# One square per token tile over both banks, in place of one per bank, in a four-layer transformer kernel

## The reference, cut to what matters

```
x = x + rms_norm(f(rms_norm(x, g_pre)), g_post)       (some with a factor 0.5 before the second norm)
rms_norm(y, g) = y * rsqrt(mean(y*y) + 1e-6) * g      (mean over the 1024 columns)
```

## Time and profile before

| | |
|---|---|
| median of 3 runs | 1870.45 us (1869.24 to 1873.09) |
| the profiled execution | 1869.73 us |
| its span | 1867.9 us |
| PE busy | 1818.2 us, 97% of the span |
| DVE busy | 1113.2 us, 60% |
| ACT busy | 913.2 us, 49% |
| POOL busy | 73.7 us, 4% |
| mean granted clock of PE | 0.992 |

### The profile page before, as it was taken

How to read it: one execution, slowest core, us unless ns; L and a number is a source line. 1 busy time by engine, 2 the same in 40 slices (tenths; PEclk the granted TensorE clock), 3 DMA queues, 4 the chain that set the end, 5 groups by cost and what they waited for, 6 DMA issues and landing times.

```text
span 1867.9 us, 21863 instructions
## 1 busy us (share of the span) xinstructions
PE 1818.2 (97%) x8662; PEld 1513.4 (81%) x8662; DVE 1113.2 (60%) x1457; ACT 913.2 (49%) x1378; POOL 73.7 (4%) x184
## 2 busy tenths in 40 slices
PE   5998999999999999999999999999999999999998
PEld 5897888888788878888888878887888888878887
DVE  6775655776655565556566755556555666674554
ACT  4555444655444454445454444444444545454443
POOL 1001000200000010001000000001000100000000
PEclk9999999999999999999999999999999999999999
DMA  6434555634455565556455555655555655555552
GB/s 206 136 115 135 192 191 174 184 120 133 137 191 191 180 209 186 182 194 208 161 184 196 164 176 184 194 185 192 192 190 181 206 177 180 187 175 164 190 187 91
DMA packets 221206, 327.80 MB, mean 175 GB/s; under 512 B 10544, under 2 KB 156528, under 8 KB 220848
## 3 DMA queue, kind: packets, MB, share of 16 engines
q1 hardware_dynamic: 218592, 318.64, 52.3%
q0 software_dynamic: 1952, 7.67, 1.3%
q10 hardware_dynamic: 560, 0.08, 0.0%
HBM read 325.31 MB, written 1.05 MB: 175 GB/s over the span
## 4 chain that ended last, share of the span: by engine, by line
PE 96%; DVE 2%; ACT 1%; issue 1%; DMA 0%; ACTq 0%; DVEq 0%; POOLq 0%; POOL 0%
PE Dp L1714 16%; PE Dp L1716 16%; PE Dp L1715 16%; PE Gp L1714 13%; PE Gp L1716 13%; PE Gp L1715 13%; PE Tp L1773 2%; DVE wlo L1041 1%; PE Gp L1896 1%; PE Tp L1887 1%; PE Dp L1920 1%; PE Tp L1729 0%; PE Tp L1920 0%; PE Dp L1896 0%; DVE stage L1101 0%
## 5 line engine op out<-in xcount | busy, mean ns | idle before, releaser
L1041 DVE TENSOR_TENSOR wlo<-raw,whi 128x1024 fp32r<-128x1024 f32 (+1 forms) x608 | 715.0, 1214 | 367.1 <-ACT whi L614 367.0
L614 ACT ACTIVATE whi<-raw 128x1024 fp32r<-128x1024 f32 (+1 forms) x608 | 606.5, 1045 | 308.8 <-PE Dp L1716 164.3
L1714 PE MATMUL Gp<-whi,a_hi 128*128 128x512 f32 x1056 | 422.4, 400 | 19.6 <-DVE inner L1142 19.6
L1716 PE MATMUL Gp<-whi,a_lo 128*128 128x512 f32 x1056 | 414.6, 393 | 0.0
L1715 PE MATMUL Gp<-wlo,a_hi 128*128 128x512 f32 x1056 | 414.0, 392 | 0.0
L1714 PE MATMUL Dp<-whi,a_hi 128*128 128x512 f32 (+2 forms) x672 | 257.2, 383 | 14.4 <-ACT Z L757 7.0
L1716 PE MATMUL Dp<-whi,a_lo 128*128 128x512 f32 (+2 forms) x672 | 252.0, 375 | 0.0
L1715 PE MATMUL Dp<-wlo,a_hi 128*128 128x512 f32 (+2 forms) x672 | 251.4, 374 | 0.0
L1714 PEld LDWEIGHTS Gp<-whi,a_hi 128*128 128x128 f32 x1056 | 200.0, 189 | 61.3 <-DVE inner L1142 22.2
L1716 PEld LDWEIGHTS Gp<-whi,a_lo 128*128 128x128 f32 x1056 | 199.8, 189 | 43.2
L1715 PEld LDWEIGHTS Gp<-wlo,a_hi 128*128 128x128 f32 x1056 | 200.4, 190 | 39.7
(11 more groups left out here) (246 smaller groups left out, 1623.4 us busy)
## 6 DMA issues: line engine op xcount, KB each, us to landing
raw<-in_ffn_w_gate_up SPq DMA_DIRECT2D x176, 512.0 KB, 4.7
raw<-in_w_in SPq DMA_DIRECT2D x132, 512.0 KB, 4.6
raw<-in_ffn_w_down SPq DMA_DIRECT2D x88, 512.0 KB, 4.4
raw<-in_w_gate SPq DMA_DIRECT2D x44, 512.0 KB, 4.0
raw<-in_w_up SPq DMA_DIRECT2D x44, 512.0 KB, 5.0
raw<-in_w_down SPq DMA_DIRECT2D x44, 512.0 KB, 4.3
raw<-in_w_out SPq DMA_DIRECT2D x16, 512.0 KB, 4.1
raw<-in_w_pool_out SPq DMA_DIRECT2D x16, 512.0 KB, 4.3
```

Of the source, the lines that this page charges most:

```text
L614: return nc.scalar.activation(whi[g % W][0:rows, c0:c0 + n], raw[g % R][0:rows, c0:c0 + n], ACT.Copy).then_inc(hi_done, 1)
L1041: return V.tensor_tensor(wlo[g % W][0:rows, c0:c0 + n], raw[g % R][0:rows, c0:c0 + n], whi[g % W][0:rows, c0:c0 + n].bitcast(F32), ALU.sub ...
L1714: mm(o, hi, wh, start=start, stop=False, skip_group_check=True)
L1716: return mm(o, lo, wh, start=False, stop=stop, skip_group_check=True)
```

## The change

`square_y` loses its index c. It waits for `done[t]`, the end of both halves, and squares 1024 columns over both banks of the tile in one ACTIVATE with one accumulator. So there are 20 squares in place of 40. `scaled(t, 0)` and `scaled(t, 1)` both wait for this one square. POOL adds eps to the one sum and takes the power: two instructions a tile in place of three. PE's increments of `y_c0` go away. The order of the calls on every engine stays, but for the two squares that become one.

```diff
             def y_rstd(t, s):
                 eps = EPS * (4.0 if s in HALVED else 1.0)
-                pool.wait_ge(ysq[t], 2 * s + 1)
-                pool.tensor_scalar(ssy[:, 2 * t:2 * t + 1], ssy[:, 2 * t:2 * t + 1], eps, None, ALU.add
-                                   ).then_inc(ysum[t], 1)
-                pool.wait_ge(ysq[t], 2 * s + 2)
-                pool.wait_ge(ysum[t], 2 * s + 1)
-                pool.tensor_tensor(sy[:, t:t + 1], ssy[:, 2 * t:2 * t + 1], ssy[:, 2 * t + 1:2 * t + 2], ALU.add
-                                   ).then_inc(ysum[t], 1)
-                pool.wait_ge(ysum[t], 2 * s + 2)
+                pool.wait_ge(ysq[t], s + 1)
+                pool.tensor_scalar(sy[:, t:t + 1], ssy[:, t:t + 1], eps, None, ALU.add).then_inc(ysum[t], 1)
+                pool.wait_ge(ysum[t], s + 1)
                 pool.tensor_tensor(rsy[:, t:t + 1], sy[:, t:t + 1], half[:, 0:1], ALU.pow).then_inc(yrs[t], 1)
...
-            def square_y(t, c, s, last):
-                if c == 1:
-                    act.wait_ge(done[t], used(last))
-                elif s in BY_CHUNK:
-                    act.wait_ge(done[t], used(last - 2))
-                else:
-                    act.wait_ge(y_c0[t], c0_of(s))
-                i = 2 * t + c
-                nc.scalar.activation(junk[:, 512 * i:512 * i + 512], D(t, c), ACT.Square,
-                                     scale=1.0 / 16 if s in HALVED else 1.0 / 32, accum_out=ssy[:, i:i + 1]
+            def square_y(t, s, last):
+                act.wait_ge(done[t], used(last))
+                nc.scalar.activation(junk[:, DM * t:DM * t + DM], Dp[:, DM * t:DM * t + DM], ACT.Square,
+                                     scale=1.0 / 16 if s in HALVED else 1.0 / 32, accum_out=ssy[:, t:t + 1]
                                      ).then_inc(ysq[t], 1)
...
-                square_y(0, 0, s, last)
-                square_y(0, 1, s, last)
+                square_y(0, s, last)
...
-                square_y(1, 0, s, last)
-                square_y(1, 1, s, last)
+                square_y(1, s, last)
...
             def scaled(t, c, s):
-                dve.wait_ge(ysq[t], 2 * s + c + 1)
+                dve.wait_ge(ysq[t], s + 1)
...
-                        ins.then_inc(y_c0[t] if c == 0 else done[t], 1)
+                    ins.then_inc(done[t], 1)
...
-                            if last:
-                                ins.then_inc(y_c0[t], 1)
```

More of the change, by code:

```diff
@@ L292, in build @@
         x_out = sem("x_out")
-        y_c0, ysq, ygd = two("y_c0"), two("ysq"), two("ygd")
+        ysq, ygd = two("ysq"), two("ygd")
         ysum, yrs, xr = two("ysum"), two("yrs"), two("xr")
```

## The result

Before: 1871.4 us (median of 4, 1869.2 to 1873.1). Changed: 1888.1 us (median of 4, 1886.8 to 1888.8). Ratio 1.0089, 95% interval 1.0077 to 1.0102: slower by 16.7 us. The forecast was 1884.8, with a range of 1880 to 1889.5. The profiled executions took 1869.73 and 1886.83 us; their spans, 1867.9 and 1885.0, differ by 17.1.

The account below looks back on a forecast made before the run. PE was taken as the bound (96% of the chain), its restart set by tile 1's DVE sequence. 9.87 + 1.24 + 0.32 + 0.42 + 0.70 = 12.6, with the clock 14.4 us: 1884.8 us, range 1880 to 1889.5.

Parts of the forecast that it names:

- the clock: Stretches of PE at half clock after its gaps: +1.8 us, bounds -1.8 to +9.0.
- The head of tile 1's chain: Tile 1's first `scaled` waits for the whole-tile square; `mult` and PE restart 1.41 us later at seven passages, 9.87 us.
- the passage into the second attention: Counted at 1.41 us like the feed-forward passages, perhaps 0.15 us less because its lo has 712 columns.
- The second mixer's passages: At two passages PE's transposes of tile 1 wait for the later residual: 0.62 us each, 1.24 in all.
- Tile 0 and the last stage: Later squares delay the first mixer's softmax (+0.42 us), the last stage's PE (+0.32) and the kernel's end (+0.70).
- POOL: Taking away one POOL addition a tile (0.2 us), which ran before the second square ended, is worth nothing.
- POOL would block DVE: Rival: POOL's power delays the lo between tile 1's two `scaled` by 0.3 us, 2.7 us more, 1887.5; chance 0.08.
- seven should give seven: +1.8 us: Seven PE gaps above 3.1 us should give seven stretches at half clock, against six before: +1.8 us.
- second sign of being wrong: The prediction is wrong if the granted clock changes by more than three stretches at half clock.
- one stretch per gap above 3.1 us: Five PE gaps above 3.1 us had given five stretches at half clock, so seven should give seven.
- the clock falls oftener: Rival: gaps of 4.4 us give two half-clock stretches each, four more than taken, +7.2 us, 1892; chance 0.10.
- The price: Each stretch at half clock after a PE gap costs 1.8 us at most, 0.09 of a 20 us window.

Follow-up runs that it names:

- e2: Kernel before with one square over both banks for tile 1 alone, tile 0 keeping one per bank: 1885.8 us, ratio 1.0067.
- e4: Changed kernel with DVE doing tile 1's second lo ahead of both `scaled` in place of between them: 1878.5 us, ratio 1.0033 to the kernel before.
- e8: Kernel before with one lo of tile 1 moved behind the `mult`, except before the second mixer: 1859.4 us, ratio 0.9928.
- e1: Kernel before with one square over both banks for tile 0 alone, tile 1 keeping one per bank: 1874.6 us, ratio 1.0013.
- e7: Kernel before with POOL's addition of eps in the norm of y left out, one instruction a tile: 1871.95 us, ratio 1.0000.
- e5: Kernel before with 10 discarded matmuls ahead of PE's wait for the `mult` at each of six feed-forward passages: 1862.4 us, ratio 0.9947.
- e6: Changed kernel with 10 discarded matmuls ahead of PE's wait at the six feed-forward passages: 1880.5 us, ratio 1.0044 to the kernel before.
- e3: Kernel before with two 512-column squares per tile kept, both waiting for the end of the whole tile: 1884.9 us, ratio 1.0062.

## Why the prediction was right

The forecast held for time, direction and chain. One term of it, the clock, was mis-sized by a factor of three, and that the sum still fell into the range is owed to bounds set wide enough for it.

**How the 17.1 us divide.** The two profiled executions have the same 8662 matmuls in the same order, so each can be set against its partner. For the passage from stage 3 to 4 these are the last product of tile 1, the restart (675.44 and 682.49, above) and the 25th matmul from there. Before:
```profile
670.30 0.40 PE L1716 MATMUL Gp<-whi,a_lo 128*128 128x512 f32 x1
...
680.83 0.39 PE L1715 MATMUL Gp<-wlo,a_hi 128*128 128x512 f32 x1
```
Changed (the partner of the first is the product of 675.95 above):
```profile
689.49 0.39 PE L1702 MATMUL Gp<-wlo,a_hi 128*128 128x512 f32 x1
```
The distance goes from 5.65 to 7.05 us at the restart, which is the chain's 1.4, and on to 8.66, which is the clock's 1.6. Done for the whole program, six passages bear 1.41 us each, the one into the second attention 1.31, the two into the second mixer 1.31 together, the softmax 0.37, `turn_f` 0.37, the last stage 0.7: the chain is 12.5 us. The clock is 5.6. The start gives back 0.95, for the most part because PE waited 2.6 us for a parameter's first transfer and 3.8 before, a wait that ran from 2.4 to 4.2 us over the other runs.

**The head of tile 1's chain** was right in place and size. Square to `scaled` 1.15 us (worked out 1.15), the square 1.024 us (1.01), PE's end to residual 3.49 (3.48 to 3.49), to the `mult` +1.41. Seven passages bear it, and e2, e4 and e8 show it from three sides. At the passage into the second attention it was 0.10 us less, for which the prediction had allowed 0.15. The prediction explains why 1.79 us at the head become 1.42 by a 0.15 us wait for POOL and a 0.1 us wait for PE's transposes; by the starts in the earlier trace rows these two are 0.22 and 0.15 us. Its 1.42 was worked out from the starts and is right.

**The second mixer's passages**: the list of waits has the new wait of tile 1's transposes for the residual at eight passages. In the passage shown the first four follow PE's last product (675.95) after 0.63 us, where products follow one another after 0.23, and the second four after another 0.66 in place of 0.44 (670.54 to 670.98 before): 0.40 + 0.22 = 0.62 us, as worked out. The two passages into the second mixer took 0.66 and 0.65.

**Tile 0 and the last stage**: the softmax makes PE's transposes wait 0.46 us, and of this 0.2 is left at the product behind them, which is what had been worked out. `turn_f` came 0.37 us late (0.32 worked out), the last residual 0.70. e1, which has just the first two, measured +2.5 us, with an interval of 0.4 to 4.3 that includes the 0.7 forecast.

**POOL** was worth nothing, by e7. That POOL would block DVE is refuted: the power ran from 673.80 to 674.37, the lo of 674.05 took its usual 1.22 us. (e7 leaves out the addition ahead of the second square; no run tests POOL's two instructions behind it.)

**The clock** is the term that was mis-sized: "seven should give seven: +1.8 us". There were eleven stretches, not seven, and they cost 5.6 us more than those of before. The prediction's own second sign of being wrong, a granted clock that changes by more than three stretches, came true: it changed by five. What failed is the step that counted one stretch per gap above 3.1 us: of the four gaps of 4.4 us three had two, and so had one of 3.2. The rival "the clock falls oftener" had named this number, four stretches more, and held it as 0.10. But it is no rule either: e2, with the same gaps, had six stretches, and e7, with the gaps of before, had eight where the kernel before had six. That the rival's count was hit is in part luck. Why the same gap is followed by none, one or two is left open by these runs.

The price was wrong too, in the other direction. From the restart to the 25th matmul, at the six passages into a feed-forward, PE needs 5.4 us where no stretch follows (twice in the kernel before), 6.7 to 7.0 with one and 7.7 to 8.1 with two: 1.3 to 1.6 us for one, 2.3 to 2.7 for two, in place of 1.8 for each. A part of a stretch can lie in the gap, where PE does nothing. Eleven stretches against six at 1.8 us would have been +9.0; they were +5.6.

**The sum's zero**: I had added 0.7 us for the distance of the profiled execution to the median of 3; the fourth run moved that median to 1871.4, another 0.9. That is part of the 3.3 us by which the forecast was low. The rest is the difference itself, 16.7 us in place of 14.4: the clock took 3.8 more than its term, and the start of the profiled pair gave 0.95 back.

## What to carry to other kernels

A reduction that follows a matmul in halves is not two instructions too many: the first half runs while the producer is still at the second, and merging them moves the start of everything behind it to the producer's end. Before merging, look at what the in-order engine behind does between the halves, and count a delay at its head, less the idle gaps that it swallows on the way, wherever that engine's sequence releases the bottleneck: here 1.41 us of 1.79. And when a gap on TensorE grows, price the clock behind it as well, with a wide range: here it made a third of the loss, its share varied between executions with the same gaps, and filling the gaps with discarded matmuls won 9 us in the kernel before.

## What the runs showed of the hardware that I had not expected

Discarded matmuls in the idle gaps raised the granted clock from 0.992 to 0.999 and made the kernel before 0.5% faster (e5), with no other change; a gap of 2.1 us still let it fall at three of four passages (e6), and the gaps left by the filling, 1.4 us at most, at none (e5, one profile). In that profile the unfilled gap of 3.2 us had none behind it either, and gaps of one length were followed by no, one or two stretches in different executions (e2 and the changed kernel, e7 and the kernel before).

A POOL addition of one column, 0.20 us alone, took 1.25 us when it was issued 0.01 us after a DVE subtraction with two SBUF inputs (e3), and so became the last thing that the residual waited for. In the other direction nothing showed: of 608 such subtractions in the changed kernel none took more than 1.227 us, the nine that started inside a power of the y norm among them:
```profile
L1028 DVE TENSOR_TENSOR wlo<-raw,whi x608: 659/1219/1227, 12.7 to 1864.0; 128x1024 fp32r<-128x1024 f32 x149, 128x712 fp32r<-128x712 f32 x2, 128x512 fp32r<-128x512 f32 x1
```

A square of 1024 columns over two PSUM banks (1.024 us) took 0.43 us more than one of 512 over one bank (0.593), and the step from 512 to 1024 columns is 0.42 us for the casts: nothing measurable was paid for the second bank.
